# Modulation products in four column groups, exp in place of the Silu and Gelu tables, and bias rows turned earlier

## The reference, cut to what matters

```python
def _modulation(cond, w, b):                  # cond: c and c_ctx, two rows of 1024
    m = jax.nn.silu(cond) @ w + b             # w (1024, 6144), once per layer of the second block
    return jnp.split(m[:, None, :], 6, axis=-1)

def compress(t, pos, w1, w2):                 # in the attention, for keys and for values
    blocks = t[:, cmp_idx] + pos
    return jax.nn.gelu(blocks.reshape(b, n_cmp, CMP_LEN * d) @ w1) @ w2
```

## Time and profile before

| | |
|---|---|
| median of 3 runs | 2565.36 us |
| the profiled execution | 2571.6 us, its span 2569.8 us |
| PE busy | 2414.7 us, 94% of the span |
| DVE busy, ACT busy | 1368.0 us (53%), 1196.1 us (47%) |
| the modulation's matmuls (L770) | 173.5 us busy, 768 records |
| mean granted TensorE clock | 0.979 |

### The profile page before, as it was taken

One profiled execution on the slowest core, in us unless ns is written; L12 is line 12 of the kernel. 1 busy time (PEld: TensorE's weight loads), 2 busy tenths in 40 slices (PEclk: granted clock), 3 DMA queues, 4 the chain that ended last, 5 costly groups with the idle time before them and its releaser, 6 DMA issues.

```text
span 2569.8 us, 33587 instructions
## 1 busy us (share of the span) xinstructions
PE 2414.7 (94%) x13404; PEld 1927.8 (75%) x13404; DVE 1368.0 (53%) x2356; ACT 1196.1 (47%) x2101; POOL 0.2 (0%) x4
## 2 busy tenths in 40 slices
PE   7999999999999999899999999898999997899997
PEld 6744999974489987678867767676777885658987
DVE  3534565553466556544555555346666436446664
ACT  4533554553355447444433434225555323544663
POOL 0000000000000000000000000000000000000000
PEclk9999999999999999999999999999999998999999
DMA  6753354575335532222212211121222221303442
GB/s 242 262 181 115 133 187 172 181 274 183 117 131 183 179 131 82 82 83 98 99 49 75 73 49 67 65 82 66 99 82 99 99 99 54 110 17 134 172 162 92
DMA packets 45144, 312.27 MB, mean 122 GB/s; under 512 B 4759, under 2 KB 6935, under 8 KB 8004
## 3 DMA queue, kind: packets, MB, share of 16 engines
q1 hardware_dynamic: 44996, 310.19, 34.1%
HBM read 309.09 MB, written 1.07 MB: 121 GB/s over the span
## 4 chain that ended last, share of the span: by engine, by line
PE 84%; DVE 7%; ACT 5%; issue 2%; DMA 1%; SPq 0%; ACTq 0%; DVEq 0%
PE bank L653 55%; PE bank L658 8%; PE bank L770 7%; DVE ws L1399 2%; PE bank L674 2%; ACT ws L1013 2%; PE bank L900 2%; DVE xs L1415 1%; PE bank L810 1%; PE bank L870 1%; PE bank L882 1%; PE bank L913 1%; PE bank L791 1%; PE bank L755 1%; PE bank L754 1%
## 5 line engine op out<-in xcount | busy, mean ns | idle before, releaser
L653 PE MATMUL bank<-xs,ws 128*128 128x256 f32 (+1 forms) x9840 | 1618.9, 327 | 85.7 <-issue 39.4
L653 PEld LDWEIGHTS bank<-xs,ws 128*128 128x128 f32 x9840 | 1446.6, 193 | 262.2 <-issue 56.4
L1399 DVE TENSOR_TENSOR ws<-ring,ws 128x1024 fp32r<-128x1024 f32 x464 | 547.8, 1222 | 308.2 <-ACT ws L1013 307.7
L1013 ACT ACTIVATE ws<-ring 128x1024 fp32r<-128x1024 f32 x464 | 464.6, 1049 | 298.4 <-PE bank L653 280.7
L1415 DVE TENSOR_TENSOR xs<-arena,xs 128x512 fp32r<-128x512 f32 (+1 forms) x286 | 161.9, 581 | 315.1 <-ACT xs L1029 314.4
L1029 ACT ACTIVATE xs<-arena 128x512 fp32r<-128x512 f32 (+1 forms) x286 | 149.0, 539 | 335.3 <-PE bank L653 220.5
L1029 ACT ACTIVATE xs<-hT 128x256 fp32r<-128x256 f32 (+1 forms) x328 | 165.5, 518 | 283.0 <-PE bank L653 207.4
L1415 DVE TENSOR_TENSOR xs<-hT,xs 128x256 fp32r<-128x256 f32 (+1 forms) x328 | 177.8, 551 | 187.1 <-ACT xs L1029 185.5
L658 PE MATMUL bank<-ws,xs 128*128 128x512 f32 (+1 forms) x1008 | 232.8, 392 | 16.9 <-DVE ws L1399 7.9
L658 PEld LDWEIGHTS bank<-ws,xs 128*128 128x128 f32 x1008 | 191.4, 192 | 57.5 <-DVE ws L1399 9.8
L770 PE MATMUL bank<-arena,cs 128*2 128x256 f32 x768 | 173.5, 379 | 0.1
(11 more groups left out here) (211 smaller groups left out, 1392.8 us busy)
## 6 DMA issues: line engine op xcount, KB each, us to landing
ring<-in_stream SPq DMA_DIRECT2D x233, 1024.0 KB, 4.8
arena<-in_side SPq DMA_DIRECT2D x56, 1024.0 KB, 4.8
arena<-in_tokens SPq DMA_DIRECT2D x1, 2048.0 KB, 12.2
arena<-bias_vectors SPq DMA_DIRECT2D x1, 1536.0 KB, 7.7
out<-arena SPq DMA_DIRECT2D x1, 1024.0 KB, 4.1
arena<-in_params SPq DMA_DIRECT2D x1, 918.0 KB, 7.8
arena<-bias_vectors SPq DMA_DIRECT2D x1, 706.0 KB, 9.1
con<-in_consts SPq DMA_DIRECT2D x1, 447.5 KB, 3.2
```

What stands on the lines that cost most here:

```text
L653: ins = mm(ps(n, 0, g.T), a[wi][:, p * P:(p + 1) * P], x[xi], start=first, stop=last)
L1013: do(ws[:, i % 2, 0, c], ring[:, w % R, c], ACT.Copy).then_inc(w_high, 1)
L1399: ins = v.tensor_tensor(ws[:, i % 2, 1, c], ring[:, w % R, c], ws[:, i % 2, 0, c].bitcast(F32), ALU.subtract)
```

## The change

- The modulation products of a turn go to four groups of 32 columns of the array, product k to group k mod 4, so that each group sums two of the eight. The stationary operand is 32 columns wide, of which 30 are zero. ScalarE copies all 128 partitions of the bank (L1138), and in place of the two transposes, two float32 products with a constant matrix (`strips`) sum the four groups and turn the rows at once.
- In turns 1 and 2 of each layer, TensorE issues six float32 products of 128 by 128 by 128 with constant operands (`keep_warm`) ahead of its wait for the copied rows.
- The silu of the conditions is made of an exponential on ScalarE and an addition, a reciprocal and a product on VectorE, early in layer 0's first `proj` group. The gelu is made of four operations of VectorE, an exponential of ScalarE, and three more of VectorE in turn 1. No other table than that of exp and ln is loaded in the first block.
- The bias rows are turned head by head between the chunks of layer 0's second `proj` group, as 24 smaller copies.

```diff
@@ tensor @@
+            def keep_warm(n, at, cols, count):
+                for _ in range(count):
+                    mm(ps(n, at, at + cols), ones, con[:, 0:cols], start=True, stop=True)
...
                         if i < ADA_W:
                             for k in range(KD):
-                                ins = mm(bank[n % BANKS][0:2, 0:T], cs[:, 2 * k:2 * k + 2], wd[:, k, :],
-                                         start=(k == 0), stop=(k == KD - 1))
+                                c = 32 * (k % 4)
+                                ins = mm(bank[n % BANKS][c:c + 32, 0:T], cs[:, k, :], wd[:, k, :],
+                                         start=(k < 4), stop=(k >= 4))
                         if i:
+                            if i <= 2:
+                                keep_warm(n, 384, 128, 6)
                             pe.wait_ge(mod_rows, seen(mod_rows))
                             for g in range(2):
-                                ins = nc.tensor.transpose(ps(n, T + 2 * g, T + 2 * g + 2),
-                                                          arow[:, (i - 1) % 2, g * P:(g + 1) * P], ident[0:2, 0:2])
+                                ins = mm(ps(n, T + 2 * g, T + 2 * g + 2), arow[:, (i - 1) % 2, g * P:(g + 1) * P],
+                                         con_at("strips", 2), start=True, stop=True)
@@ scalar @@
+                if l == 0:
+                    do(hid[:, 0, :], par_at("cond", 0, 16), ACT.Exp, scale=-1.0).then_inc(cond_exp, 1)
...
-                if l == 0:
-                    do(cs[:, :], par_at("cond", 0, 16), ACT.Silu).then_inc(cs_ready, 1)
-                    exp_ln_tables()
...
-                for i in range(4):
-                    act_.wait_ge(bank_free[N(("hidT", l)) % BANKS], N(("hidT", l)) // BANKS + 1)
-                    do(hidg[:, i, :], hid[:, i, :], ACT.Gelu_apprx_tanh, bias=hid[:, i, 15:16]).then_inc(hid_ready, 1)
-                exp_ln_tables()
+                act_.wait_ge(gelu_arg, l + 1)
+                do(hid, hidg, ACT.Exp, scale=-2.0 * math.sqrt(2.0 / math.pi)).then_inc(gelu_exp, 1)
...
-                        do(arow[:, i % 2, :], bank[n % BANKS][0:2, 0:T], ACT.Copy).then_inc(mod_rows, 1)
+                        do(arow[:, i % 2, :], ps(n, 0, T), ACT.Copy).then_inc(mod_rows, 1)
@@ vector @@
+                if l == 0:   # after normed(): add 1, reciprocal, product with cond into cs[:, :, 0:2]
...
+                if l == 0:
+                    first = G("proj", l, 0).q0 + KD
+                    dve.wait_ge(dma_bias, 32)
+                    for b in range(12):
+                        feed_to(first + b // 2)
+                        v.tensor_copy(bias[:, b, 0:128], hankel[:, b, 0:128][:, ::-1])
+                        v.tensor_copy(bias[:, b, 128:384], hankel[:, b, ::-1])
...
+                gx = lamp.rearrange("p (a b) -> p a b", a=4)   # add, square, scale and add, product -> hidg
...
-                    v.tensor_copy(bias[:, :, 0:128], hankel[:, :, 0:128][:, :, ::-1])
-                    v.tensor_copy(bias[:, :, 128:384], hankel[:, :, ::-1])
...
                 for i in range(NU + 1):
+                    if i == 1:   # after gelu_exp: add 1, reciprocal, product with gx -> hidg, hid_ready
```

More of the change, by code:

```diff
@@ L146, in consts_layout @@
     p.add("pick", 127)
+    p.add("strips", 2)
     return p
@@ L406, in build @@
         x3 = region(o("x3"), (2, 16, 16))
-        arow = region(o("x3"), (2, T))[0:2]
+        arow = region(o("x3"), (2, T))
         vn = region(o("vn"), (3, 2, T))
@@ L439, in build @@
         mod = sb("mod", [P, DEPTH, 96])
-        cs = sb("cs", [P, 16])
+        cs = sb("cs", [P, KD, 32])
         scrap = sb("scrap", [P, DEPTH])
@@ L523, in build @@
         gate_exp = sem("gate_exp_ready")
+        cond_exp = sem("condition_exp_ready")
+        gelu_arg = sem("gelu_argument_ready")
+        gelu_exp = sem("gelu_exp_ready")
         lam_sum = sem("lambda_sums_ready")
@@ L726, in _ @@
                     if i == CMP_AT:
-                        pe.wait_ge(hid_ready, seen(hid_ready, 4))
+                        pe.wait_ge(hid_ready, seen(hid_ready))
                         n = N(("kc", l))
@@ L996, in _ @@
             exp_ln_tables()
-            act_.wait_ge(small_ready, 2)
+            act_.wait_ge(small_ready, 3)
             act_.wait_ge(dma_par, 32)
@@ L1436, in _ @@
             v.memset(one[:, :], 1.0).then_inc(small_ready, 1)
+            v.memset(cs[:, :, :], 0.0).then_inc(small_ready, 1)
             v.memset(cbias, NEG).then_inc(dve_own, 1)
@@ L1449, in _ @@
                 normed(("g_attn", l), G("proj", l, 0))
+                if l == 0:
+                    dve.wait_ge(cond_exp, 1)
+                    v.tensor_scalar(hid[:, 0, :], hid[:, 0, :], 1.0, None, ALU.add).then_inc(dve_own, 1)
+                    dve.wait_ge(dve_own, own(dve_own))
+                    v.reciprocal(hid[:, 0, :], hid[:, 0, :]).then_inc(dve_own, 1)
+                    dve.wait_ge(dve_own, own(dve_own))
+                    v.tensor_tensor(cs[:, :, 0:2], par_at("cond", 0, 16).rearrange("p (a b) -> p a b", a=KD),
+                                    hid[:, 0, :].rearrange("p (a b) -> p a b", a=KD), ALU.mult).then_inc(cs_ready, 1)
                 dve.wait_ge(lam_exp, seen(lam_exp))
@@ L1456, in _ @@
                 dve.wait_ge(dve_own, own(dve_own))
+                if l == 0:
[5 more added lines that the diff above has]
+                        v.tensor_copy(bias[:, b, 128:384], hankel[:, b, ::-1])
+                    for q in range(2):
+                        ins = v.tensor_copy(cbias[:, :, 16 * q:16 * q + CMP_N], tz[:, :, P * q:P * q + 225:16][:, :, ::-1])
+                    ins.then_inc(cbias_ready, 1)
                 for i in range(2):
@@ L1477, in _ @@
                 v.tensor_copy(hid.rearrange("p a b -> p (a b)"), ps(n, 0, 64)).then_inc(bank_free[n % BANKS], 1)
+                dve.wait_ge(bank_free[n % BANKS], n // BANKS + 1)
+                gx = lamp.rearrange("p (a b) -> p a b", a=4)
+                v.tensor_tensor(gx, hid, hid[:, :, 15:16].to_broadcast([P, 4, 16]), ALU.add).then_inc(dve_own, 1)
+                dve.wait_ge(dve_own, own(dve_own))
+                v.tensor_tensor(hidg, gx, gx, ALU.mult).then_inc(dve_own, 1)
+                dve.wait_ge(dve_own, own(dve_own))
+                v.tensor_scalar(hidg, hidg, 0.044715, 1.0, ALU.mult, ALU.add).then_inc(dve_own, 1)
+                dve.wait_ge(dve_own, own(dve_own))
+                v.tensor_tensor(hidg, hidg, gx, ALU.mult).then_inc(gelu_arg, 1)
                 dve.wait_ge(gate_exp, seen(gate_exp))
@@ L1484, in _ @@
                 gates = lam[:, 16:40].rearrange("p (a b) -> p a b", a=2)
-                if l == 0:
-                    dve.wait_ge(dma_bias, 32)
-                    v.tensor_copy(bias[:, :, 0:128], hankel[:, :, 0:128][:, :, ::-1])
-                    v.tensor_copy(bias[:, :, 128:384], hankel[:, :, ::-1])
[L1490 to L1493, removed]
-                for i in range(NU + 1):
+                dve.wait_ge(cbias_ready, 1)
+                for i in range(NU + 1):
+                    if i == 1:
+                        dve.wait_ge(gelu_exp, l + 1)
+                        v.tensor_scalar(hid, hid, 1.0, None, ALU.add).then_inc(dve_own, 1)
+                        dve.wait_ge(dve_own, own(dve_own))
+                        v.reciprocal(hid, hid).then_inc(dve_own, 1)
+                        dve.wait_ge(dve_own, own(dve_own))
+                        v.tensor_tensor(hidg, hid, gx, ALU.mult).then_inc(hid_ready, 1)
                     if i < NU:
@@ L1912, in pack_constants @@
     put("pick", pick)
+    put("strips", np.tile(np.eye(32, 2), (4, 1)))
     t = np.arange(T)
```

## The result

The changed kernel takes 2456.93 us (median of 4 runs, 2456.39 to 2457.63) against 2565.69 us for the kernel before: a ratio of 0.957 with a 95% interval of 0.956 to 0.959, 108.8 us less. The forecast was 2464 us, in a range of 2448 to 2490. The profiled execution took 2456.7 us, its span is 2454.9 us. The kernel before, timed again beside the experiments, had medians of 2570.26 to 2572.41 us, so the size of the gain is known to some 6 us only.

The account below looks back on a forecast made before the run. TensorE was taken to bound modulated attention turns. From the profiled 2571.6 us, -121.9 + 16.3 + 8.2 - 4.2 + 0.1 = -101.5 gave 2470.1 us, or 2464 us from the median; range 2448 to 2490.

Parts of the forecast that it names:

- The bound: Modulated attention turns: TensorE alone forms the chain of waits, 5.88 us a turn, so time taken from it shortens the kernel.
- The products: Modulation products in 48 turns: 3.54 us becomes 1.00 us a turn (0.88 to 1.30), removing 121.9 us.
- The sum: Two float32 products replacing two transposes in each of 48 turns: +0.34 us a turn, 16.3 us in all.
- A drain at the change of tiling mode: Sum step in 48 turns: no price seen; one drain of 0.10 us a turn would lose 5 us more.
- The extra products: Turns 1 and 2 of each layer: 2.0 us a turn, 8.2 us added in all, 6.6 to 9.8.
- The tables: Layer 0 between `proj` and `nat`: without two table loads and the low clock, 4.2 us gained, between 2.6 and 4.5.
- The entry: Attention's entry: gelu loads and bias-row turning lose their 3.54 us modulation cover, but are gone too; no wait left.
- The bias rows in `proj`: Layer 0's `proj`: smaller copies fit VectorE's 2.73 us of waiting a slot, costing nothing; 6.5 us if wholly exposed.
- The other engines and the transfers: Modulated turns: ScalarE, VectorE and side-weight transfers (2.5 to 3.2 us) all stay below TensorE's new 3.68 us turn.
- the copy out of PSUM may take over: Rival in modulated turns: evacuation sets 4.2 us turns, 2486 us; 12 in 100 together with side weights taking 4.2 us.
- the column groups do not overlap: Rival in the modulation products: they still take 3.54 us, so the kernel ends slower at 2586 us; 3 in 100.
- The clock: Rival in attention: short bursts and more waiting drop TensorE to 1.2 GHz, some 2620 us; 2 in 100.

Follow-up runs that it names:

- the whole transposes: Changed kernel with two transposes of the whole 128 by 128 copy replacing the two float32 sum products: 2451.26 us; also without the extra products: 2450.18 us.

## Why the prediction was right, point by point

**The bound.** TensorE alone in the chain of a modulated turn: right, and right after the change too. The kernel without the groups shows that nothing else shortened attention, which is 52.3 us a layer shorter where 48 were forecast.

**The products.** 1.00 us a burst was taken, between 0.88 and 1.30; measured 1.00 in the chain. The compression's burst in the same trace was the right row.

**The sum.** +0.34 us a turn was taken; measured 0.54 - 0.21 = +0.33. A drain at the change of tiling mode, which the Trainium skill states (TensorEngine Tiling (Array Packing), Key Properties), shows no price of its own: the pieces of the changed turn, with stationary operands of 32, 64 and 128 columns, lie end to end within 0.02 us. The prediction read 32 columns from the earlier trace rows already; the modulation's operand there is 2 columns wide.

**What was not in the sum.** The unit's transposes became 0.10 us shorter in the turns that have three of them: some 2 us a layer. That is a term I had no row for.

**The extra products.** Mis-sized twice. They take 1.53 us a turn and the sum behind them 0.34, 1.87 together, where I had 2.0 + 0.55: 0.68 us less in each of four turns, 2.7 us. And I priced them as fully on the path, with 2 us kept for the range. Taken out, they bring 1.1 us a layer, since ScalarE's copies take their place. By the chains 108.8 us went where 101.5 were forecast, 7.3 us more; the shorter transposes, some 4 us, and these 2.7 are nearly all of it. That the medians differ from the forecast by the same 7 us is in part luck, since the median of the kernel before moved by 5 to 7 us from one measurement to the next.

**The tables.** 4.2 us by the difference of the layers: measured 4.2 in the stretch of layer 0 both ways (23.86 us when the table is put back), and 5.0 in the median.

**The entry.** "This cover is gone; but the work is gone too" is shown: with the work put back it costs 4.4 us in the median, 3.0 of attention in layer 0 and 0.3 in layer 1. The forecast of that run, 1 to 2 us a layer, had the wait and not the clock that falls behind it.

**The bias rows in `proj`.** Nothing was taken. The two `proj` groups last 45.12 us in the chain of the changed kernel and 46.27 before; eleven profiles with the bias rows there lie between 45.05 and 46.42 us, three without them between 45.91 and 46.29. So no cost shows that is larger than this spread.

**The other engines and the transfers.** No limit at 3.57 us was forecast: right. The warning that the copy out of PSUM may take over after a fourfold gain (the Trainium skill, the same page, PSUM Bottleneck) did not come true at this turn length, with VectorE at 40.30 us and ScalarE at 35.58 of 68.50.

**The rivals.** That the column groups do not overlap is refuted by the burst. The clock was given 2 in 100, on the ground that TensorE kept 1.00 while busy in only 5.08 of 7.00 us. The result bears the number out, but the ground was bad: a stretch of 7 us with waits is no evidence for 80 us of lighter turns, and with half of the products the clock fell behind 20 us with TensorE busy in all of them. The runs show how near it was. Without the extra products four of ten executions fall, and with half of the products all four do. I took `keep_warm` for a cost alone. By the counts, none of 28 executions with it against four of ten without, it is what keeps the changed kernel at 2457 us each time; no trace shows how.

**Open.** What work of the array in a turn is enough was not found; nor in which turn the clock falls in the executions without extra products (no profile of one is at hand); nor whether the whole transposes protect against it. That each 68 us step is one layer's attention at the low clock is argued, not shown: with half of the products layer 1 ran at 0.50 from turn 3 nearly to the end of attention and took 49 us longer than in the changed kernel, and full bursts would lose more.

## What to carry to other kernels

Price a new form of product from the same form elsewhere in the trace, as bursts of like length, and look again at the pieces behind it. When work on the bound engine is cut, ask what it covered, at the entry of the loop above all. And when TensorE's work in a loop gets lighter, look at the granted clock over many executions and not only at the median: a busy share of 100% does not show that it will hold.

## What the runs showed of the hardware that was not expected

- Half of the modulation products made the kernel 78 us slower: the clock fell from 1.00 to 0.50 in a stretch where TensorE was busy in 5.00 of 5.00 us, and in the next layer stayed at 0.50 through 40.00 of 40.00 busy us. Two constant float32 products a turn (0.64 us in the chain) held it at 1.00.
- In that execution the same turn with the same wait of 0.51 us kept 1.00 in layer 0 and lost it in layer 1; and one kernel took 2457, 2527 or 2593 us from execution to execution.
- Eight float32 products on four column groups take 1.00 us alternating and 1.02 us in pairs of one group; 0.97 us with 2 in place of 32 stationary columns.
- Three transposes take 0.48, 0.38 or 0.33 us in the chain, behind two small transposes, behind a float32 product with a full stationary operand, or behind transposes like themselves.
